# Layer 2's experts in an order made on the chip: twelve lightly loaded ones as six pairs, and late units with the down products first

## What is computed

```python
def hier_moe(h, w_group, w_expert, w_gate, w_up, w_down):
    g_prob = softmax(t @ w_group)                 # 4 groups, the best one is taken
    e_logits = (t @ w_expert)[own group]          # 8 experts in a group, the best two are taken
    ...
    for e in range(32):
        he = silu(t @ w_gate[e]) * (t @ w_up[e])  # 1024 -> 256
        y = y + combine[:, e, None] * (he @ w_down[e])   # 256 -> 1024
# per layer: x = x + g_m * mixer(h);  x = x + g_f * hier_moe(h);  at the end rmsnorm(x)
```

## Time and profile before

| | us |
|---|---|
| median of the runs | 692.44 |
| span of the profiled execution, first to last instruction | 690.7 |
| PE busy | 651.0 (94%) |
| DVE busy | 251.7 (36%) |
| ACT busy | 121.3 (18%) |
| POOL busy | 64.9 (9%) |
| read from HBM | 271.59 MB, 395 GB/s over the span |

### The profile page before, as it was taken

The page is one execution under the profiler, slowest core; times in us unless marked ns, Lnnn a source line. Parts: engine busy times, 40 slices in busy tenths (PEclk is TensorE's granted clock), DMA queues, the critical chain, the costliest instruction groups (busy, mean ns, idle before and its releaser), DMA issues.

```text
span 690.7 us, 13056 instructions
## 1 busy us (share of the span) xinstructions
PE 651.0 (94%) x4864; PEld 399.9 (58%) x4864; DVE 251.7 (36%) x661; ACT 121.3 (18%) x317; POOL 64.9 (9%) x187
## 2 busy tenths in 40 slices
PE   4889899998899999999999999999999999999995
PEld 1445465554554555557888788877555555555552
DVE  1014423222222223235689495255322232232233
ACT  4013530000000000014234323237000000000003
POOL 7000021101001011100000000001111111011000
PEclk9999999999999999999999999999999999999998
DMA  9999999999999999999997989963999999999981
GB/s 354 418 422 422 427 419 438 428 431 426 431 428 431 433 428 426 423 421 420 417 422 280 417 339 425 422 280 136 419 428 422 425 427 426 421 424 427 423 357 64
DMA packets 27256, 273.31 MB, mean 396 GB/s; under 512 B 3140, under 2 KB 3652, under 8 KB 4936
## 3 DMA queue, kind: packets, MB, share of 16 engines
q1 hardware_dynamic: 27208, 272.65, 94.3%
HBM read 271.59 MB, written 1.05 MB: 395 GB/s over the span
## 4 chain that ended last, share of the span: by engine, by line
PE 86%; DMA 9%; issue 2%; ACT 1%; SPq 1%; DVE 1%; ACTq 0%; DVEq 0%
PE bank L760 77%; DMA ring<-in_ada_w_dram 9%; PE bank L968 8%; PE bank L1361 1%; SPq L468 0%; ACT hx L1849 0%; PE bank L1215 0%; PE bank L1222 0%; DVE ye L1890 0%; ACT reg_b L1653 0%; ACTq L164 0%; DVE ye L1887 0%; SPq L562 0%; DVE keep L1890 0%; ACT reg_b L1698 0%
## 5 line engine op out<-in xcount | busy, mean ns | idle before, releaser
L760 PE MATMUL bank<-ring,xh 128*64 128x256 f32 (+1 forms) x2496 | 332.9, 421 | 13.4 <-issue 12.6
L760 PEld LDWEIGHTS bank<-ring,xh 128*64 128x64 f32 x2496 | 185.1, 137 | 116.5 <-issue 50.5
L714 POOL COPY xh<-reg_a 128x256 f32 (+1 forms) x130 | 51.6, 397 | 451.0 <-PE bank L760 316.9
L1563 ACT ACTIVATE reg_c<-bank 128x128 f32<-128x128 f32 x64 | 17.7, 277 | 390.9 <-PE bank L760 390.9
L1887 DVE TENSOR_TENSOR reg_c<-reg_c,bank 128x128 f32<-128x128 f32 x64 | 18.4, 287 | 178.6 <-ACT reg_c L1563 178.6
L968 PE MATMUL bank<-ye,reg_b 32*128 32x512 f32 (+1 forms) x528 | 64.3, 600 | 0.0
L760 PE MATMUL bank<-reg_b,ring 128*128 128x256 f32 x256 | 57.2, 380 | 0.4 <-ACT reg_b L1698 0.4
L1887 DVE TENSOR_TENSOR ye<-bank,reg_c 128x512 f32<-128x512 f32 (+1 forms) x66 | 44.3, 671 | 32.4 <-PE bank L760 32.0
L2100 DVE COPY xh<-bank 128x128 f32<-128x128 f32 x64 | 18.2, 285 | 96.0 <-PE bank L760 96.0
L760 PEld LDWEIGHTS bank<-reg_b,ring 128*128 128x128 f32 x256 | 48.0, 190 | 7.1 <-issue 0.9
L760 PE MATMUL bank<-ring,cact 128*32 128x512 f32 (+1 forms) x320 | 34.1, 536 | 16.4 <-DMA ring<-in_ada_w_dram 16.1
(11 more groups left out here) (183 smaller groups left out, 402.2 us busy)
## 6 DMA issues: line engine op xcount, KB each, us to landing
ring<-in_exp_w_dram SPq DMA_DIRECT2D x41, 2048.0 KB, 17.3
ring<-in_exp_w_dram SPq DMA_DIRECT2D x20, 3072.0 KB, 16.0
ring<-in_ada_w_dram SPq DMA_DIRECT2D x48, 1024.0 KB, 17.7
ring<-in_exp_w_dram SPq DMA_DIRECT2D x44, 1024.0 KB, 18.3
ring<-in_w_qkv_dram SPq DMA_DIRECT2D x12, 1024.0 KB, 16.2
ring<-in_w_o_dram SPq DMA_DIRECT2D x4, 1024.0 KB, 8.7
gu_spare<-in_exp_w_dram SPq DMA_DIRECT2D x1, 2048.0 KB, 20.2
hx<-in_exp_w_dram SPq DMA_DIRECT2D x2, 1024.0 KB, 19.7
```

The costliest lines, as they stand in the source:

```text
L714: nc.gpsimd.tensor_copy(xe[:, b, k0:k1, t * CAP:(t + 1) * CAP], hS[:, k0:k1, bass.ds(off, CAP)])\
L760: return nc.tensor.matmul(o_, l_, r_, start=start, stop=stop)
L1563: nc.scalar.activation(sil[:, b, :], bank[b][:, 0:P], ACT.Silu).then_inc(S("sil_ready", L), 1)
```

## The change

All of it is in layer 2's MoE.

1. **Places.** After routing, DVE computes for each expert from 7 to 31 a place: those with at most 16 tokens in both tiles come first (`order_experts`). A product on PE (`order_rows`) turns this round into the expert and the two list offsets of each place, and DVE writes them where SP and POOL read them (`places_by_rows`). Experts 0 to 6 keep their places. SP loads `order_i[place]` into a register ahead of each gate and up load.
2. **Units.** PE, DVE, ACT and POOL now walk over 26 units: places 0 to 3, then pair (7,8), 4, pair (9,10), 5, pair (11,12), 6, the pairs (13,14), (15,16), (17,18), then places 19 to 31 alone. In a pair each expert has 16 slots per tile, so that its 32 stationary columns fill a quarter of the array's width. The experts with buffers of their own are now 4, 5 and 6.
3. **Table.** A second form of the table of output rows (`tab_light`) is made for the pairs: two products of 128 columns in place of four of 32; DVE derives the old form from it by four copies.
4. **Late units.** From unit 14 on (`LATE`) PE makes the down product of the unit before ahead of this unit's gate and up.
5. **Room for overflow**: 4 levels in place of 3, with a capacity for each expert.

```diff
+LIGHT = CAP // T
+NLP = 6
+STAT = 7
-ALONE = ({R: R}, {10: R, 17: FREED, 24: SPARE})
+ALONE = ({R: R}, {4: R, 5: FREED, 6: SPARE})
+LIGHTS = [(STAT + 2 * n, STAT + 2 * n + 1) for n in range(NLP)]
+UNITS = [(0,), (1,), (2,), (3,), LIGHTS[0], (4,), LIGHTS[1], (5,), LIGHTS[2], (6,)] + LIGHTS[3:] \
+    + [(p,) for p in range(STAT + 2 * NLP, E)]
+LATE = NU - 12
...
# SP
+            sp.wait_ge(S("off_ready"), 3)
+            e = expert_of(STAT)
+            gate_up(1, e, *exp_at(1, STAT))
+            for p in range(STAT, E):
+                if p + 1 < E:
+                    following = expert_of(p + 1)
+                    gate_up(1, following, *exp_at(1, p + 1))
+                down_part(1, e, *exp_at(1, p))
...
# PE
+            def order_rows():
+                pe.wait_ge(S("diag_ready"), T + 1)
+                pe.wait_ge(S("hS_dve"), 2 * len(BY_DVE))
+                mm(order_at, ones[0:E, :], order_diag, True, True).then_inc(S("counts"), 1)
...
+                    table_light(0)
+                    table_light(1).then_inc(S("tab_full"), 1)
...
+                    for k in range(KC):
+                        for x in range(2):
+                            for j in range(2):
+                                g = CAP * (2 * x + j)
+                                last = mm(bank[b][g:g + CAP, 0:F], xe[:, b, k, x * CAP:(x + 1) * CAP], w[x][:, k, j, :, :],
+                                          k == 0, k == KC - 1)
...
+            def late_unit(u):
+                b = u % 2
+                if u > LATE:
+                    rows_unit(u - 2, b)
+                turn_he_of(1, u - 1, 1 - b)
+                if u == LATE:
+                    rows_unit(u - 2, b)
+                down_unit(u - 1, 1 - b, True)
+                hidden_unit(u, b)
+                if u == NU - 1:
+                    rows_unit(u - 1, 1 - b)
+                    turn_he_of(1, u, b)
...
# DVE, in route(1)
+                    nc.vector.memset(hS[:, :, NSLOT:PAD], 0.0).then_inc(S("hS_pad"), 1)
+                    order_experts()
...
+                if L:
+                    take_gathered(L)
                 for t in range(T):
                     tt(diag[:, t, :, :], ident.unsqueeze(1).broadcast_to([P, 4, P]),
...
+                    places_by_rows()
...
+            def order_experts():
+                free = slice(STAT, E)
+                nc.vector.tensor_scalar(place_of, of_expert, 1.0 / RANKS, None, ALU.mult)
+                then(nc.vector.tensor_scalar(fits, cnt[:, E + STAT:2 * E], float(LIGHT), None, ALU.is_le))
+                then(stt(fits, cnt[:, free], float(LIGHT), fits, ALU.is_le, ALU.mult))
+                then(nc.vector.tensor_tensor_scan(fit_n, ones[:, 0:ND], fits, 0.0, ALU.mult, ALU.add))
...
+                then(nc.vector.tensor_reduce(of_place_sum, of_place, AX, ALU.add))
+                tt(order_diag, ident[0:E, 0:E].unsqueeze(1).broadcast_to([E, 3, E]),
+                   of_place_sum.unsqueeze(2).broadcast_to([E, 3, E]), ALU.mult).then_inc(S("diag_ready"), 1)
```

More of the change, by code:

```diff
@@ L620, in _ @@
             up_part(1, early, R)
[L621 to L627, removed]
+            sp.wait_ge(S("off_ready"), 3)
[6 more added lines that the diff above has]
+                down_part(1, e, *exp_at(1, p))
+                e = following
+                if p == STAT + 1:
                     sp.wait_ge(S("tab_full"), 2)
@@ new lines, in down_unit @@
+            def down_unit(u, b, clear):
+                pe.wait_ge(S("heT_ready", 1), u + 1)
+                w = []
+                for p in UNITS[u]:
+                    s, fill = loaded(1, p)
+                    w.append(down_w(s))
+                    pe.wait_ge(S("ring_last", s), down_full(1, s, fill))
+                if clear:
+                    pe.wait_ge(S("ye_ready", 1), u - 1)
+                waited()
+                if len(w) == 1:
+                    last = down(bank[2 + b], w[0], b)
+                else:
+                    for j in range(2):
+                        for half in range(2):
+                            for x in range(2):
+                                g, c = CAP * (2 * half + x), CAP * (2 * x + j)
+                                last = mm(bank[2 + b][g:g + CAP, :], heT[:, b, c:c + CAP],
+                                          w[x][:, j, half * 512:half * 512 + 512], j == 0, j == 1)
+                last.then_inc(S("dn_ready", 1), 1)
@@ new lines, in rows_unit @@
+            def rows_unit(u, b):
+                if len(UNITS[u]) == 1:
+                    add_rows_of(1, u, b)
+                    return
+                pe.wait_ge(S("share_ready", 1), u + 1)
+                pe.wait_ge(S("ye_ready", 1), u + 1)
+                waited()
+                for t in range(T):
+                    for half in range(2):
+                        rows = slice(64 * half, 64 * half + 64)
+                        last = nc.tensor.matmul(bank[4 + half + 2 * t][:, :], share_light[rows, b, t, :], ye[rows, b, :],
+                                                start=False, stop=False, skip_group_check=True)
+                last.then_inc(S("rows_added", 1), 1)
@@ L1206, in _ @@
             gather(0)
-            for e in range(FRONT[0]):
+            for e in range(FRONT):
                 expert_at(0, e)
@@ L1482, in _ @@
             gather(1)
-            for e in range(FRONT[1]):
+            order_rows()
+            for e in range(2):
                 expert_at(1, e)
@@ L2120, in take_ye, with match_unit @@
                 gated(ye[:, b, :], bank[2 + b][:, :]).then_inc(S("ye_ready", L), 1)
+            def match_unit(u, first=False):
+                places = UNITS[u]
+                if not first:
+                    dve.wait_ge(S("share_ready", 1), u)
+                if len(places) == 1:
+                    stt(hit, tab[:, 0:2 * P], lanes[:, places[0]:places[0] + 1], tab[:, 2 * P:4 * P], ALU.is_equal, ALU.mult)\
+                        .then_inc(S("matched", 1), 1)
+                    return
+                n = LIGHTS.index(places)
+                for t in range(T):
+                    stt(hit_light[:, t, :], tab_light[:, t, 0:2 * P], light_lanes[:, t, n:n + 1], tab_light[:, t, 2 * P:4 * P],
+                        ALU.is_equal, ALU.mult).then_inc(S("matched", 1), 1)
@@ new lines, in share_unit, with expert_unit @@
+            def share_unit(u, b):
+                dve.wait_ge(S("matched", 1), sum(T if len(v) == 2 else 1 for v in UNITS[:u + 1]))
+                if len(UNITS[u]) == 1:
+                    last = tt(share[:, b, :], hit[:, 0:P], hit[:, P:2 * P], ALU.add)
+                else:
+                    last = tt(share_light[:, b, :, :], hit_light[:, :, 0:P], hit_light[:, :, P:2 * P], ALU.add)
+                last.then_inc(S("share_ready", 1), 1)
+            def expert_unit(u):
+                b = u % 2
+                if u:
+                    take_heT(1, u - 1, 1 - b)
+                if u == 1:
+                    dve.wait_ge(S("tab_ready"), 2)
+                    for g in range(4):
+                        rows = slice(32 * g, 32 * g + 32)
+                        nc.vector.tensor_copy(tab[rows, :], tab_light[rows, g % T, :]).then_inc(S("tab_ready"), 1)
+                if u == 2:
+                    dve.wait_ge(S("tab_ready"), 6)
+                    dve.wait_ge(S("gf_ready"), 2)
+                if u >= 2:
+                    match_unit(u - 2, first=u == 2)
+                    if b == 0:
+                        if u > 2:
+                            dve.wait_ge(S("rows_added", 1), u - 3)
+                        take_ye(1, u - 2, 0)
+                    share_unit(u - 2, b)
+                gate_he(1, u, b)
+                if u == 0:
+                    count_beyond(1)
+                if u >= 2 and b == 0:
+                    if u > 2:
+                        dve.wait_ge(S("rows_added", 1), u - 2)
+                    take_ye(1, u - 1, 1)
@@ L2414, in _ @@
             route(1)
-            for e in range(FRONT[1]):
-                expert_at(1, e)
-                if e == 0:
-                    count_beyond(1)
             later_experts(1)
```

297 lines of the change are left out of this document (228 added, 69 removed).

## The result

| | before | changed |
|---|---|---|
| median of 6 runs, us | 692.51 (692.43 to 692.6) | 694.79 (693.24 to 695.27) |
| ratio, 95% interval | | 1.0029 (1.0017 to 1.0040) |
| span of the profiled execution | 690.7 | 692.0 |

The account below looks back on a forecast made before the run. Layer 2's experts were taken as bound by loads at 425 GB/s as well as by PE. End -2.3, ordering +0.46 and table +0.15 gave -1.7 us: 692.44 to 690.8 us; 689.4 to 692.9 held 8 in 10.

Parts of the forecast that it names:

- the one on the late units: Last units and end: PE waits for the previous unit's down part; PE ends at 680.7 instead of 683.0, gaining 2.3 us.
- its cover is the wait itself and the following units' 1 us each: Clock falling in waits ahead of units 11 and 12: gate and up 3.7 us longer, the sum unchanged.
- The loads' rate: Layer 2's expert loads: DMA engines full at 425 GB/s from 500 to 665 us, 7.40 us per expert.
- What pairs cost on PE: Each of six pairs on PE: about 7.7 us against 12.9 for two singles; at worst 13.
- DVE's ordering: Ahead of the first expert: 2.9 us on DVE, making the first gate and up 0.46 us late (0 to 1.2).
- The 0.15 for the table: Table's two longer products: second load 0.7 us later, of which 0.15 us was charged (0 to 0.7).
- The stretch behind the last gate and up: End of layer 2's experts: from the last gate and up's end at 675.6 to PE's end, 5.1 us.
- The parenthesis that the old order would leave more: End of the experts: in the old order the last gate and up could begin at 667.7.
- The waits ahead of units 11 and 12: PE, once the stock of loaded experts is used up: waits of some 5 to 7 us before each of these units.
- The signs of being wrong: GB/s below 415, first issue after 480.5, or last gate and up not right behind a down product that waited for its load.
- Rival 3: Late singles: the clock stays at 1.2 GHz at the end, giving 699 us; chance 0.04.
- rival 1: Same within 0.2%: front costs more, end gives 0.3 less, 692.3 us; chance 0.35.

Follow-up runs that it names:

- Run 10: Changed kernel with the turn ahead of the added rows in all late units, not only the first: 699.06 us, ratio 1.0089.
- run 1: Changed kernel with pairs kept, but every unit and the end in the order of before: 690.24 us, ratio 0.9969.
- run 9: Changed kernel with idle PE products ahead of the waits of units 11 and 12 and at the late units' entry: 693.81 us, ratio 1.0017.
- run 3: Changed kernel with idle PE products ahead of the two long waits, of units 11 and 12: 694.88 us, ratio 1.0029.
- run 4: Changed kernel with DVE taking the gathered rows directly behind the ordering: 693.65 us, ratio 1.0015.
- run 5: Changed kernel with 12 idle PE products at the entry of the late units (unit 14) alone: 693.74 us, ratio 1.0019.
- run 11: run 8 with the idle PE products of run 3 ahead of units 11 and 12: 688.97 us, ratio 0.9950.
- run 7: Changed kernel with the edits of run 1 and run 4 together: 689.54 us, ratio 0.9959.
- run 8: run 7 with one set of added rows moved ahead of the last gate and up: 688.82 us, ratio 0.9947.
- run 2: Changed kernel with the new order only in the last two units instead of the last twelve: 692.08 us, ratio 1.0001.

## Why the prediction was wrong

**The step that failed** is the one on the late units: "PE now waits in each unit for the down part of the unit before". I had put the work of a unit (6.43 us) beside its loads (7.40) and taken a 1 us reserve per unit from it, as if the order did not matter. But 6.43 us holds only where DVE's copy of the turned rows, and ACT's and DVE's work on gate and up, lie under PE's own work. With down ahead of gate and up nothing lies between the turn and the product that needs it: 0.39 us of turn, then PE standing for 0.47 while DVE copies, and rows alone to cover silu. The unit takes 7.32. Run 10 shows it to be the pace by making it 7.78, and run 1 by taking it away: the same pairs, loads and front end 4.5 us earlier. So the reserve is not 1 us per unit but 0.08 beside the forecast's 7.40, and 0.16 beside the 7.47 at which the parts landed here, and most of a lag at unit 14 is still there at the end.

**What I did not have in the sum** is the entry of the late units. Unit 14 began its down product 4.2 us after it could (593.4 for 589.2): ahead of it stand two sets of pair rows (3.7 us), the turn, 2.36 us for DVE and 2.0 for one more set. Over the eleven units that follow 1.7 were given back (4.19 less 2.46). Prediction against the profile: 689.0 + 0.6 (the loads landed later than forecast) + 2.4 = 692.0.

**The remaining 1 us of the median and the 2 us of spread** are the granted clock, as far as idle products can show it: with them at all three waits both are gone (run 9). Among the traced executions with the 2.36 us at the entry the clock fell there in one (run 3) and not in three (the changed kernel, runs 4 and 10); and it stays low for different lengths ahead of units 11 and 12 (run 5). I had priced the fall at nothing with "its cover is the wait itself and the following units' 1 us each"; runs 1 and 11 show that this is right where the units have that reserve, and the late order had taken it away. The Trainium skill, TensorE: Matmul & The Clock Gate, section "HAM oscillation — how this bites in real kernels", says that DMA waits of a few us let the clock fall, so that the next piece of work starts slow. The traces agree: the clock is 0.50 as unit 11's gate and up begins, behind 9.1 us of waiting. In rows 8 the clock fell some 2.1 us behind PE's last product (683.0; 0.57 over 685 to 686), not the 2.4 I wrote.

**Right, with sizes:**
- The loads' rate: 424 GB/s from 500 to 660; the last gate and up lands at 668.8 (668.2 forecast), the down part at 671.4 (670.8). The first load left 1.2 us later than before (480.71 for 479.51), and the last part landed 1.2 later, so the last landing did move only with the first issue. In runs 1, 7, 8 and 11 they do set the end.
- PE without a wait for loads until 548.6 (about 550 forecast).
- What pairs cost on PE: in run 3, at full clock, gate, up and down of a pair take 5.38 us, as a single's; 64-row added rows 1.92 (1.9 forecast).
- DVE's ordering took 2.89 us (470.36 to 473.25; 2.9 forecast). The first gate and up was 0.85 us late after the 0.2 common to all, not 0.46: 0.64 from DVE (0.46 summed) and 0.21 from POOL, whose copy took 0.50 us for 0.29. The 0.15 for the table was not seen: the other 0.15 us of the first load's 1.2 lie between the end of that gate and up and SP's issue (0.29 us, 0.14 before), where SP's register loads now stand, which I had put at nothing; that they are the cause isn't shown. In the timeline

```profile
474.86 0.99 DVE L2275 TENSOR_SCALAR reg_a<-bank,colq 128x256 f32<-128x256 f32 x2
...
476.10 0.50 POOL L764 COPY xh<-reg_a 128x128 f32 x1 [1.89 <-ACT reg_a L1723]
...
476.75 3.67 PE L836 MATMUL bank<-ring,xh 128*64 128x256 f32 x32 [0.32 <-POOL xh L764]
```

- The stretch behind the last gate and up: 679.32 to 684.30 is 5.0 us (5.1 forecast).
- The parenthesis that the old order would leave more became the best kernel. I had that number and did not ask why the order would then still pay.

**The waits ahead of units 11 and 12** were 9.1 and 3.6 us, not 5 to 7 each; the loads set when they end.

**The signs of being wrong** that the forecast named: the first issue came later than 480.5 (480.71), and the last gate and up stood behind a down product that waited for DVE and not for its load. The second is the failed step itself. GB/s stayed at 420 or above in every 20 us from 500 to 660.

**The rivals.** None was the one. Rival 3 (the clock at the end) had the smaller of the two mechanisms, in another place; rival 1 had the slower front; the price of a chain on PE was in none.

## What to carry to other kernels

The sum of an engine's work per unit is a lower bound, and holds only for an order in which the hand-overs to other engines lie under other work. Before an order is changed so that an engine waits less for loads, write the chain of one unit with its hand-overs and compare that, not the sum, with the load. And where a queue of loads is the bound, work that can run ahead of the last load (a set of rows, run 8) is worth up to its own length (0.7 us of 1.07), while a fall of the clock inside the units cost nothing here unless their reserve was gone.

## What the hardware showed that I had not expected

- The granted clock fell from 2.4 to 1.2 GHz just behind waits of 1.98 us (run 1), 2.17 us (run 2) and 2.36 us (run 3), and did not behind one of 2.36 us in the changed kernel and in runs 4 and 10. In runs 5 and 9, 12 idle products of 128 columns (2.94 us) in place of the last kept it up. The six runs of the changed kernel stand in two groups, near 693.5 and near 695.0 us.
- Gate and up of a pair, 32 products of 32 columns by fours, took what 16 of 64 columns by twos took, to 0.01 us together with down (5.38 and 5.39); the timeline shows no gap where one form follows the other.
- POOL's copy of 128x128 took 0.50 us beside DVE's two 128x512 operations on `diag`, and 0.29 before, with DVE idle. That DVE is what slows it was not tried.
